# One attention program instead of two in the second block of a two-block layer stack, with the steps before and after it rearranged

## The reference, cut to what matters

```python
def second_block(x, mem, ...):                       # S = 512 rows, D = 1024
    h = rmsnorm(x, g_mix)
    q_a, k_a, v_a, q_i, k_i, w_i, conv_in, q_m, gate_logits = split(h @ w_in)
    # 8 query heads, 2 key heads of width 64; keys chosen by an indexer, causal
    o_a = dsa_attention(rope(rmsnorm(q_a)), rope(rmsnorm(k_a)), v_a, ...)
    o_b = conformer_conv(conv_in, ...)
    # 4 heads of width 128 over 256 memory rows, no mask
    k_m, v_m = split(rmsnorm(mem) @ w_mem_kv);  k_m = rmsnorm(k_m, g_km)
    o_m = softmax(rmsnorm(q_m, g_qm) @ k_m.T * 128 ** -0.5) @ v_m
    gates = sigmoid(gate_logits + b_gate)            # three gates of width 1024
    merged = gates[0]*(o_a @ w_br_a) + gates[1]*(o_b @ w_br_b) + gates[2]*(o_m @ w_br_m)
    x = x + merged @ w_o
    return x + hier_moe(rmsnorm(x), ...)             # 32 experts
```

## Time and profile before

| | us |
|---|---|
| median of 3 runs | 2827.54 (2826.27 to 2828.27) |
| profiled execution | 2828.22 |
| span of the profiled execution | 2826.4 |
| PE busy | 2483.8 (88% of the span) |
| DVE busy | 1483.8 (52%) |
| ACT busy | 1036.1 (37%) |
| POOL busy | 287.9 (10%) |

### The profile page before, as it was taken

The page is one execution under the profiler, slowest core; times in us unless marked ns, Lnnn a source line. Parts: engine busy times, 40 slices in busy tenths (PEclk is TensorE's granted clock), DMA queues, the critical chain, the costliest instruction groups (busy, mean ns, idle before and its releaser), DMA issues. The chain is left out here.

```text
span 2826.4 us, 34000 instructions
## 1 busy us (share of the span) xinstructions
PE 2483.8 (88%) x12483; PEld 2032.4 (72%) x12483; DVE 1483.8 (52%) x2217; ACT 1036.1 (37%) x1736; POOL 287.9 (10%) x288
## 2 busy tenths in 40 slices
PE   5999996688999898998899898799697788599995
PEld 4777785576888775766688786687486567599994
DVE  4766445545555434634555534367896654433333
ACT  3422332334444335323544433433334523033332
POOL 0000001100000000000000000455240250001111
PEclk9999998899999998999999999899898899699997
DMA  4122232122333321203233322222020021699995
GB/s 139 68 82 90 90 105 75 60 75 61 103 94 106 127 77 61 90 30 104 60 90 103 117 106 75 70 100 90 30 90 30 23 90 52 217 367 372 378 370 212
DMA packets 212860, 330.59 MB, mean 117 GB/s; under 512 B 13861, under 2 KB 109997, under 8 KB 212749
## 3 DMA queue, kind: packets, MB, share of 16 engines
q1 hardware_dynamic: 208013, 312.33, 32.2%
q0 software_dynamic: 4736, 16.78, 2.0%
HBM read 299.99 MB, written 29.10 MB: 116 GB/s over the span
## 5 line engine op out<-in xcount | busy, mean ns | idle before, releaser
L366 PE MATMUL ps<-ffn_h_hi,ffn_w_hi 128*128 128x512 f32 x704 | 275.8, 392 | 10.5 <-DVE ffn_h_lo L361 10.5
L367 PE MATMUL ps<-ffn_h_lo,ffn_w_hi 128*128 128x512 f32 x704 | 275.4, 391 | 0.0
L368 PE MATMUL ps<-ffn_h_hi,ffn_w_lo 128*128 128x512 f32 x704 | 275.1, 391 | 0.0
L366 PE MATMUL ps<-wo_hi,lhs_hi 128*128 128x512 f32 x608 | 242.3, 399 | 34.0 <-DVE lhs_lo L361 34.0
L3865 PEld LDWEIGHTS ps<-expert_x,ring 128*128 128x128 f32 x2048 | 238.3, 195 | 8.1 <-DVE expert_x L3948 3.4
L3865 PE MATMUL ps<-expert_x,ring 128*128 128x96 f32 x2048 | 238.1, 278 | 3.8 <-DVE expert_x L3948 3.0
L367 PE MATMUL ps<-wo_lo,lhs_hi 128*128 128x512 f32 x608 | 240.5, 395 | 0.0
L368 PE MATMUL ps<-wo_hi,lhs_lo 128*128 128x512 f32 x608 | 240.3, 395 | 0.0
L361 POOL TENSOR_TENSOR w_lo<-ring,w_hi 128x512 fp32r<-128x512 f32 (+1 forms) x112 | 159.3, 1424 | 762.1 <-ACT w_hi L518 761.2
L361 DVE TENSOR_TENSOR wo_lo<-ring,wo_hi 128x1024 fp32r<-128x1024 f32 x76 | 93.0, 1223 | 184.8 <-ACT wo_hi L653 184.8
L2245 DVE SCALAR_TENSOR_TENSOR y_tmp<-ps,pcol,y_tmp 128x511 f32<-128x511 f32 x88 | 61.9, 745 | 220.1 <-ACT y_tmp L2217 220.1
(11 more groups left out here) (622 smaller groups left out, 5269.7 us busy)
## 6 DMA issues: line engine op xcount, KB each, us to landing
ring<-in_w_up SPq DMA_DIRECT2D x32, 2048.0 KB, 11.1
ring<-in_ffn_w_up SPq DMA_DIRECT2D x88, 512.0 KB, 4.9
moe_down<-in_w_down SPq DMA_DIRECT2D x32, 1024.0 KB, 6.7
ring<-in_ab_w_in SPq DMA_DIRECT2D x13, 2048.0 KB, 8.0
ring<-in_w_in SPq DMA_DIRECT2D x11, 2048.0 KB, 7.8
ring<-in_ffn_w_down SPq DMA_DIRECT2D x10, 2048.0 KB, 7.8
ring<-in_c_w_in SPq DMA_DIRECT2D x6, 2048.0 KB, 8.0
expert_results<-expert_y SPq DMA_DIRECT2D x32, 384.0 KB, 7.4
```

The lines of the kernel that those rows point to most:

```text
L366: nc.tensor.matmul(out, left[0], right[0], start=start, stop=False, **more)
L367: nc.tensor.matmul(out, left[0], right[1], start=False, stop=False, **more)
L368: return nc.tensor.matmul(out, left[1], right[0], start=False, stop=stop, **more)
```

## The change

- `head_norm_tm` and the small program that turned `km` are gone. `km` now lies in `score`. Its norm is in `heads`, ahead of the first wait there, in the shadow of the large `project`, with its square root on ACT after output 1 of that program. Its eight transposes are four more tiles at the end of `turn_heads`.
- `attend` is replaced by `attends`: one program of 48 units in the order causal, causal, memory. Scores have three PSUM banks in place of four, the turned tiles two, the causal outputs two, the memory outputs one. A memory score is no longer copied by DVE: ACT exponentiates it out of PSUM, so its bank is free only after the exponential (`k.sa`), while a causal one is free after DVE's pass (`k.va`). DVE, not ACT, copies a turned memory tile out of PSUM.
- `qm` is turned ahead of it, in place, by `turn_both`. Both outputs are turned after it in one program of eight tiles.
- In `merge`, POOL has nothing left. DVE makes the remainders, mixed with the bias additions and the gating.

```diff
+def attends(k, causal, memory, s, pt):
+    A, M = causal, memory
+    units = []
+    for t in range(NT):
+        for h in range(M.heads):
+            units += [(A, t, 2 * h), (A, t, 2 * h + 1), (M, t, h)]
...
+    SB, TB, AV, MV = 0, 3, 5, 7
...
             def scores(n):
-                t, h = units[n]
-                if n >= 4:
-                    pe.wait_ge(*k.va(n - 3))
+                kind, t, h = units[n]
+                if n >= 3:
+                    pe.wait_ge(*(k.va if units[n - 3][0] is A else k.sa)(n - 2))
...
-                if bias is None:
-                    nc.vector.tensor_reduce(top[:, t, h:h + 1], ps, AX.X, ALU.max)
-                    nc.vector.tensor_copy(s[:, n % 4, 0:keys_of(t)], ps)
...
+                    nc.vector.tensor_reduce(stat(0, n), ps, AX.X, ALU.max)
...
+            def copy_out(n):
+                kind, t, h = units[n]
+                if kind is M:
+                    dve.wait_ge(*k.pb(n + 1))
...
+                    nc.vector.tensor_copy(pt[:, n % 2, 0:kind.keys_of(t)], k.ps[:, TB + n % 2, 0:kind.keys_of(t)]).then_inc(k.da.sem, 1)
...
+            due = {last_of[kind.heads, t] + 3: (kind, t) for t in range(NT) for kind in (A, M)}
+            for n in range(len(units) + 4):
+                if n < len(units):
+                    largest(n)
+                if 2 <= n < len(units) + 2:
+                    copy_out(n - 2)
+                if n in due:
+                    read_out(*due[n])
...
+                nc.scalar.activation(scored, scored if kind is A else k.ps[:, SB + n % 3, 0:kind.keys_of(t)], ACT.Exp, bias=stat(1, n), scale=kind.scale,
+                                     accum_out=stat(2, n)).then_inc(k.sa.sem, 1)
...
 def merge(k, branches, weights, gates, bgate, m, tmp, after, held):
-        @block.gpsimd
-        def _(pool):
-            for p, (b, c) in enumerate(pieces):
-                pool.wait_ge(*k.w_hi_ready(p + 1))
-                rest(nc.gpsimd, left(1, p), branches[b][:, c, :], left(0, p))
-                rest(nc.gpsimd, w_lo[:, p % PIECES, :], raw(p), w_hi[:, p % PIECES, :]).then_inc(k.w_lo_ready.sem, 1)
-            pool.drain()
...
+            for p in range(PIECES):
+                remainders(p)
+            biased(0)
             for b in range(NB):
+                remainders(CT * b + CT - 1)
+                if b + 1 < NB:
+                    biased(b + 1)
+                    remainders(CT * (b + 1))
                 for t in range(NT):
+                    gate(b, t)
+                    if b + 1 < NB and t % 2 == 1:
+                        remainders(CT * (b + 1) + 1 + t // 2)
...
 def mixers2(k, next_gain, after):
-            head_norm_tm(k, km, km, MT, MH, MD, k.b["g_km_2"], mem)
...
             def heads(dve):
                 nc.vector.memset(u[:, :, 0:CONV_W - 1], 0.0)
+                squares = scratch[:, 0:MT * MH * MD].rearrange("p (t n) -> p t n", t=MT)
+                mean, rstd = (k.stat[:, n, 0:MT * MH].rearrange("p (t h o) -> p t h o", t=MT, o=1) for n in (0, 2))
+                nc.vector.tensor_tensor(squares, km, km, ALU.mult)
...
+                dve.wait_ge(*k.root_ready(1))
...
-        attend(k, NQ, lambda t, h: cm[:, h // 2, t * P:(t + 1) * P],
...
-        turn(k, o_tm, oa, CT)
-        qm_cm = score
-        turn(k, qm, qm_cm, CT)
-        attend(k, MH, lambda t, h: qm_cm[:, h, t * P:(t + 1) * P], lambda h, n: km_cm[:, h, 0:n], lambda t: MEM, None,
...
-        turn(k, o_tm, om, CT)
+        turn_both(k, [(qm, qm)])
...
+        attends(k, causal, memory, *spare)
+        turn_both(k, [(o_tm, oa), (score, om)])
```

More of the change, by code:

```diff
@@ L2795, in turn @@
     k.pa.close(tiles)
-def head_norm_tm(k, src, dst, tiles, heads, width, gain, sq):
+def attends(k, causal, memory, s, pt):
     nc = k.nc
[L2801 to L2832, removed]
@@ L2835, in attend @@
-def attend(k, heads, query, key, keys_of, bias, value, width, scale, o, buf):
-    nc = k.nc
-    units = [(t, h) for t in range(NT) for h in range(heads)]
-    s, pt = buf
-    SB, TB, VB = 0, 4, 6
-    top, ntop, total, rtotal = (k.stat[:, n, 0:NT * heads].rearrange("p (t h) -> p t h", h=heads) for n in range(4))
+    A, M = causal, memory
[3 more added lines that the diff above has]
+            units += [(A, t, 2 * h), (A, t, 2 * h + 1), (M, t, h)]
+    first = {(kind.heads, t): min(n for n, u in enumerate(units) if u[0] is kind and u[1] == t) for kind in (A, M) for t in range(NT)}
@@ new lines, in attends, with stat, copied @@
+    last_of = {(kind.heads, t): max(n for n, u in enumerate(units) if u[0] is kind and u[1] == t) for kind in (A, M) for t in range(NT)}
+    rank = [sum(u[0] is units[n][0] for u in units[:n]) for n in range(len(units))]
+    SB, TB, AV, MV = 0, 3, 5, 7
+    A.at, M.at = 0, NT * A.heads
+    A.bank, M.bank = lambda t: AV + t % 2, lambda t: MV
+    def stat(row, n):
+        kind, t, h = units[n]
+        at = kind.at + t * kind.heads + h
+        return k.stat[:, row, at:at + 1]
+    def copied(n):
+        return (k.sb if units[n][0] is A else k.da)(rank[n] + 1)
@@ L2844, in attend, with read @@
+    def read(kind, t):
+        return (k.vb if kind is A else k.vc)(t + 1)
     with nc.Block(no_gpsimd_drain=True) as block:
@@ L3020, in turned @@
     def turned(c):
[L3021 removed]
+        if c >= PAIRS:
+            return km_cm[:, c - PAIRS, :], k.ps[:, c % NBANKS, 0:MEM]
+        return cm[:, c, :] if c < INDEX else index[c - INDEX], k.ps[:, c % NBANKS, :]
+    tiles = PAIRS + MH
     with nc.Block(no_gpsimd_drain=True) as block:
@@ L3061, in _ @@
         def _(act):
-            for c in range(0, PAIRS, 2):
+            for c in range(0, tiles, 2):
                 act.wait_ge(*k.pa(c + 1))
-                nc.scalar.copy(turned(c), k.ps[:, c % NBANKS, :]).then_inc(k.sa.sem, 1)
+                nc.scalar.copy(*turned(c)).then_inc(k.sa.sem, 1)
     k.va.close(1)
     k.ga.close(1)
-    k.pa.close(PAIRS)
-    k.vb.close(PAIRS // 2)
-    k.sa.close((PAIRS + 1) // 2)
+    k.pa.close(tiles)
+    k.vb.close(tiles // 2)
+    k.sa.close((tiles + 1) // 2)
 def index_scores(k, index, w_idx, score, relu, between):
```

205 lines of the change are left out of this document (124 added, 81 removed).

## The result

The changed kernel has a median of 2810.94 us (2807.79 to 2814.07, 4 runs) against 2827.24 us (2826.27 to 2828.27, 4 runs) in the same session. The ratio is 0.9940, 95% interval 0.9928 to 0.9952, so the change saves 16.3 us, where I had forecast 14.7. Its profiled execution took 2814.07 us with a span of 2812.2.

What follows compares the result with a forecast made beforehand. PE, busy 88% of the span, was taken to bound both attentions, while the merge waited for POOL. Terms -8.3 - 0.8 - 5.6 = -14.7 against 2828.2 gave 2813.5, stated as 2812.8; range 2806 to 2819.

Steps and rivals of the forecast that it cites:

- Part 1: Memory keys: norm and turn moved out from in front of the large projection, -8.3 us in sum.
- The first cast: Large projection's first weight cast moves up by 9.14 us, since its program follows at once.
- The slow start: PE idles less before the large projection, so part of its slow-clock start goes: -0.5 us, between -1.4 and 0.
- `turn_heads`: Eight transposes of the memory keys added as four tiles at its end: +0.8 us, between +0.4 and +1.5.
- the collision of DVE with POOL: Large projection: three new two-input DVE operations hold up POOL's remainders; +0.5 us for all, between 0 and +2.5.
- Part 2: Attention with its turns: 76.7 us after against 77.5 before, -0.8 us, bounds -5 and +4.
- The length of a triple in tile 0: Attention, row tile 0: a DVE and ACT loop makes 2.6 us against PE's 2.20, three triples losing 0.4 each.
- Part 3: Merge: remainders on DVE and POOL silent, ending near 80.8 us in place of 86.4; -5.6 us, bounds -10 and -1.
- branch changes: Merge: PE waits for DVE's gating when the branch changes, 1.9 us at the first, 1.9 and 1.2 at the second.
- The attention is where it pays: Rival: interleaving closes idle time in the attention (-5) and merge branch changes could cost nothing (-10); 2804 us, chance 0.10.
- The gates starve the merge: Rival: merge branch changes cost twice and POOL loses its turn in the projection; 2820 us, chance 0.10.
- Three score banks: Rival: in the attention PE waits for maximum and exponential at each of 16 memory units, +21.6; 2835 us, chance 0.03.

Runs made afterwards that it cites:

- the second profile: Profile of the changed kernel run again with no edit, in a later session; 2811.56 us (6 runs), ratio 0.9944 to the kernel before.
- the kernel with this part alone: The kernel before with only the attention changed: one program of 48 units, one turn ahead and one behind; 2828.54 us (11 runs), ratio 1.0004.

## Why the prediction was right, and where not

The forecast, 2812.8, is 1.9 us above the median, inside the spread of its four runs (2807.79 to 2814.07). By the stages of the two kernels profiled first, the changed code saves 7.67 - 0.70 = 6.97 (keys), -1.04 (attention, which cost more than it saved in that execution, C and D together), and 6.52 (merge): 12.4. With the second profile it is 7.61 - 0.67 + 1.62 + 4.21 = 12.8. My sum was 14.7. The changed stages thus gave 2 us less than forecast, and some 3.5 us of the measured 16.3 come from elsewhere: the unchanged stages differ by as much from execution to execution. That the total came within 1.9 us is luck in part.

**Part 1, -8.3 predicted, -7.0 measured.** The first cast: -9.14 predicted, -9.17. The slow start: -0.5 predicted, and the third cast comes 7.23 us behind the first in place of 7.80, -0.57. `turn_heads`: +0.8 predicted, +0.70. The mis-sized term is the collision of DVE with POOL: +0.5 charged, 2.1 measured, within its range. Half of it is the two late casts, 0.60 + 0.53. The other half I had not looked for: DVE's own chain of norms and rope, from the square of the attention's columns to the last product of `qm`, sets the end of the large projection, and PE stands still for 8.3 us before the next program's first transposes (5.3 before). DVE operations in this chain met POOL where they had not, for instance:

```profile
1947.70 4.32 DVE L3033 TENSOR_TENSOR att_tm<-att_tm,brow 128x2048 f32<-128x2048 f32 x3 [0.44 <-issue]
```

Before, the same three took 3.23 us, while POOL had nothing to do. The chain took 74.09 us in place of 73.08. Both hold a wait of 16.7 us for ACT's roots; behind it the chain is 50.20 us in place of 49.17, and this 1.0 us went straight to the end.

**Part 2, -0.8 predicted, -1.6 or -1.8 at full clock, +1.0 in the first profile.** The turn of `qm` took 5.34 us (5.5 predicted). The program took 65.74 us in the second profile and in the kernel with this part alone (66.6 predicted, with 1.2 for a slow start), and 67.15 in the first, where the start was slow. The kernel before had a slow start here in all four profiles with the old attention (47.4 us each):

```profile
2158.20:2162.35 4.15, 4.15 (x19) 3.87 (x19) 2.18 (x16) 3.48 (x11) 0.00 (x0) 0.50 0.00 0
```

The 4.15 us at half clock cost about 2.1 us (an estimate), as much as the whole gain of 1.6 to 1.8. Of the ten profiles of the new program five have a stretch at half clock in row tile 0 and five have none, and why is not shown. With that stretch taken out of the old form the new one at full clock is 0.5 us longer in C and D, and with the slow start in both, and the last turn at full clock, it is 0.7 shorter. So the gain is mostly the clock's, as far as these rows tell. The last turn took 4.7 (4.6 predicted) or, with its first 16 transposes at half clock, 6.4. The sizes hold, but not all of the reasons. I wrote that interleaving cannot overlap much, and that holds. That the gain lies at the ends of the programs does not: of the 3.0 us that I read as the old causal program's edge, 2.1 are the slow clock. And interleaving has a use that I had not named: the run with the memory units last has the same ends and three waits, 1.5 us together, for the one output bank, which the mixed order hides; the rest of its 4.6 us of stage C is mostly clock. The length of a triple in tile 0 was read rightly (2.60 us), but breaking the loop gave 0.16 a triple and not 0.4, and 0.35 in tile 1, where I had put nothing.

**Part 3, -5.6 predicted, -6.5 measured** (-5.7 with the merge alone, -4.2 in the second profile, at a mean clock of 0.91). Start of PE 3.48 us after the first cast (3.4), branch changes 1.9, 1.9 and 1.0 (1.9, 1.9, 1.2), bias additions 1.22 us. The walk through the four engines held piece by piece, and moving one DVE step removed one of its waits and nothing else.

**The rivals.** *The attention is where it pays*: -5 for it, measured -1.8 at best; the merge's branch changes cost what I had said. *The gates starve the merge*: no. *Three score banks*: some 0.9 us. The measurement's own spread is the weakest part of my numbers. I had named 5.7 us as what can't be told from none, and that was not too wide: by its medians the attention is worth nothing alone and 7 us behind the other two parts.

## What to carry to other kernels

Walk each engine's fixed order through a stage with durations from rows: this gave the merge to within a microsecond where the clock was like the one before, waits included. When work is moved into the shadow of another stage, ask which engine ends that stage and whose queue the moved work's waits stand in; here it was DVE's chain, and a root on ACT in front of the casts. Compare parts by their own stages in the trace, for medians of whole executions carried some 5 us of other stages' clock.

## What the runs showed of the hardware

Code ahead of every edit began its last stage anywhere from 1768.55 to 1774.06 us, and the tail took 483.1 to 487.4, with the same instructions and more time for the same matmuls. At starts of programs the same 16 transposes took 1.94 us at full clock and up to 3.65 at half. Eight squares of the same 1024 columns in a row beside POOL took 1.15 to 2.17 us each, 13.5 together, where the ninth, with POOL silent, took 1.23. The four remainders of POOL under them took 1.5 to 2.2 us each, 7.4 together, in place of 1.3 each alone. So DVE lost about 3.7 us there and POOL 2.2.
